# A hybrid encoder layer in fp32: the attention mask moves to one engine, and the order of copies, splits and tiles changes

## What is computed

```python
h = rmsnorm(x, mix_norm_g)
q, k, v, gb, gc, u = split(h @ w_in)                 # six parts of 512 columns
attn = dilated_attention(heads(q), heads(k), heads(v), slopes)   # 8 heads of 64
conv = gb * dwconv3(gc * u)                          # 512 channels, width 3
merged = concat([rmsnorm(attn), rmsnorm(conv)])
x = x + merged @ w_out
x = x + moe_ffn(rmsnorm(x), ...)                     # top 4 of 32 experts, clamped SwiGLU
return rmsnorm(x, final_norm_g)
```

## Time and profile before

| | us |
|---|---|
| median of 3 runs | 1372.1 |
| lowest and highest | 1367.39, 1372.46 |
| the profiled execution | 1373.16 |
| its span | 1371.3 |
| PE busy | 1317.0 (96%) |
| DVE busy | 504.3 (37%) |
| GpSimd busy | 267.0 (19%) |
| ACT busy | 205.0 (15%) |

### The profile page before, as it was taken

One profiled execution on the slowest core, in us unless ns is written; L12 is line 12 of the kernel. 1 busy time (PEld: TensorE's weight loads), 2 busy tenths in 40 slices (PEclk: granted clock), 3 DMA queues, 4 the chain that ended last, 5 costly groups with the idle time before them and its releaser, 6 DMA issues.

```text
span 1371.3 us, 33077 instructions
## 1 busy us (share of the span) xinstructions
PE 1317.0 (96%) x13998; PEld 647.4 (47%) x13998; DVE 504.3 (37%) x884; ACT 205.0 (15%) x313; POOL 267.0 (19%) x258
## 2 busy tenths in 40 slices
PE   6989999988999999999999999999999999999996
PEld 5766676882444444444444444444444434444443
DVE  7456653561233222222333333322222222333335
ACT  5134433230001000000010000100000000110002
POOL 1825427024011111111111111111111111111100
PEclk9999999979999999999999999999999999999998
DMA  9322113566999999999999999999999999999984
GB/s 245 82 62 62 62 62 105 223 236 226 348 398 406 403 408 400 402 410 407 402 403 407 398 402 407 412 407 406 404 406 406 407 408 404 409 408 402 406 354 143
DMA packets 94605, 450.79 MB, mean 329 GB/s; under 512 B 12105, under 2 KB 36953, under 8 KB 45424
## 3 DMA queue, kind: packets, MB, share of 16 engines
q1 hardware_dynamic: 83280, 426.27, 77.7%
q0 software_dynamic: 8656, 19.51, 5.9%
q10 hardware_dynamic: 2640, 4.59, 0.9%
HBM read 440.08 MB, written 18.67 MB: 335 GB/s over the span
## 4 chain that ended last, share of the span: by engine, by line
PE 76%; DMA 9%; DVE 5%; issue 4%; POOL 2%; SPq 2%; ACT 1%; DVEq 0%; POOLq 0%; ACTq 0%
PE gu_bank L1551 40%; PE bank L1565 21%; DMA raw<-in_w_gate_up_dram 9%; PE bank L1316 3%; PE bank L1318 3%; PE bank L1317 3%; PE bank L1539 2%; SPq L385 2%; PE bank L1393 1%; DVE probs_a L1030 1%; PE bank L1407 1%; PE bank L1518 1%; PE bank L1568 1%; DMA x_sb<-in_x_dram 1%; DVE lo L955 1%
## 5 line engine op out<-in xcount | busy, mean ns | idle before, releaser
L1551 PE MATMUL gu_bank<-raw,xT 128*32 128x512 f32 x3072 | 341.2, 593 | 6.0 <-DMA raw<-in_w_gate_up_dram 3.1
L1212 DVE TENSOR_TENSOR gate_in<-gu_bank,b_gu 128x768 f32<-128x768 f32 x32 | 30.6, 958 | 571.1 <-PE gu_bank L1551 538.9
L1551 PEld LDWEIGHTS gu_bank<-raw,xT 128*32 128x32 f32 x3072 | 101.2, 110 | 238.9 <-issue 220.2
L1565 PE MATMUL bank<-raw_a,aT 128*32 128x256 f32 x2232 | 166.8, 380 | 0.0
L1568 PE MATMUL bank<-raw_a,aT 128*32 128x256 f32 x744 | 166.4, 380 | 0.0
L1551 PE MATMUL gu_bank<-raw_c,xT 128*32 128x512 f32 x1488 | 165.5, 592 | 0.0
L586 POOL DMA_INDIRECT sum_rows<-y_out,scatter_list x31 | 45.2, 1457 | 429.7 <-ACT y_out L852 429.7
L1237 DVE STREAM_TRANSPOSE aT<-lin_in 128x192 f32<-128x192 f32 x128 | 67.8, 532 | 143.4 <-PE bank L1568 142.3
L1565 PEld LDWEIGHTS bank<-raw_a,aT 128*32 128x32 f32 x2232 | 88.8, 110 | 62.0
L838 ACT ACTIVATE xT<-bank 128x384 f32<-128x384 f32 x66 | 28.9, 488 | 554.8 <-PE bank L1539 539.6
L1551 PEld LDWEIGHTS gu_bank<-raw_c,xT 128*32 128x32 f32 x1488 | 49.4, 110 | 110.3 <-issue 105.3
(11 more groups left out here) (240 smaller groups left out, 1628.8 us busy)
## 6 DMA issues: line engine op xcount, KB each, us to landing
raw<-in_w_gate_up_dram SPq DMA_DIRECT2D x128, 1024.0 KB
raw_c<-in_w_gate_up_dram SPq DMA_DIRECT2D x62, 1024.0 KB
raw_a<-in_w_down_dram SPq DMA_DIRECT2D x62, 1024.0 KB
raw_b<-in_w_gate_up_dram SPq DMA_DIRECT2D x32, 1024.0 KB
raw_b<-in_w_down_dram SPq DMA_DIRECT2D x32, 1024.0 KB
raw_e<-in_w_gate_up_dram SPq DMA_DIRECT2D x31, 1024.0 KB
raw_d<-in_w_down_dram SPq DMA_DIRECT2D x31, 1024.0 KB
raw<-in_w_in_dram SPq DMA_DIRECT2D x24, 512.0 KB, 5.2
```

What stands on the lines that cost most here:

```text
L1212: dve.tensor_tensor(gate_in[:, :, :], gu_bank[:, :, 0:QUARTER], gate_b, ALU.add)
L1551: ins = pe.matmul(gu_bank[c * GROUP:(c + 1) * GROUP, r, :], xT[:, i, r * GROUP:(r + 1) * GROUP], w[:, c], start=first, stop=last)
L1565: pe.matmul(bank_[c * GROUP:(c + 1) * GROUP, cols], aT[:, k, c * GROUP:(c + 1) * GROUP], w[:, at:at + QUARTER], start=first and r % 2 == 0 ...
```

## The change

- `near_ready` is gone. DVE does the whole mask: `count_branches` and `log_of(2)`, `log_of(3)`, one of them behind each of the first three takes of v. GpSimd's queue keeps the parameter loads, the biases and the convolutions.
- At p = 0, PE makes tile (4, 0) ahead of the first turns, tile (4, 1) within the turns of head 0, and nothing within those of head 1; DVE's takes follow that order.
- In the loop over pairs, ACT and DVE copy turned blocks of the first head ahead of the split of chunk s + 2. DVE's take of tile (s + 1, 0) stays between the two heads' copies for p > 0.
- Channels 0 and 1 are scaled and split into two tiles of their own, at 72 K over the probabilities of the odd heads, as soon as all turns are done: on ACT ahead of `take_pair(3)`, on DVE behind the take of tile (10, 1).

```diff
+        first_hi_m, first_lo_m = overlay(72 * K, ("first_hi_m", [P, 2, SEQ], F32R), ("first_lo_m", [P, 2, SEQ], F32R))
...
+        def m_hi(k):
+            return first_hi_m[:, k, :] if k < 2 else mT_hi[:, k, :]
...
 @@ gpsimd
-            pool.wait_ge(bits_ready, 3)
-            made(pool.tensor_scalar(seen_b[:, :], step16[:, :], 0, None, ALU.is_equal))
-            pool.wait_ge(near_ready, 2)
-            made(pool.tensor_tensor(seen[:, :], seen[:, :], seen_b[:, :], ALU.add))
-            made(pool.tensor_tensor(seen[:, :], seen[:, :], seen_c[:, :], ALU.add))
-
-            inv = HEAD_DIM ** 0.5
-            made(pool.tensor_scalar(log_m[:, :], seen[:, :], 0.0, MASKED, ALU.is_equal, ALU.mult))
-            for m in range(2, len(BRANCHES) + 1):
-                made(pool.tensor_scalar(seen_b[:, :], seen[:, :], float(m), math.log(m) * inv,
-                                        ALU.is_equal, ALU.mult))
-                pool.tensor_tensor(log_m[:, :], log_m[:, :], seen_b[:, :], ALU.add).then_inc(log_m_made, 1)
-                pool.wait_ge(log_m_made, m - 1)
...
             pool.wait_ge(params_loaded, 16 * 9)
+            pool.wait_ge(bits_ready, 3)
+            pool.wait_ge(log_m_made, 1)
...
 @@ scalar, in the loop over p
                 take(s, 1)
+                take_turned(2 * p)
                 split_front(s + 2)
-                take_turned(2 * p)
                 take_turned(2 * p + 1)
                 if p >= 2:
                     square_conv(p - 2)
+            act.wait_ge(probs_turned, HEADS * TT)
+            act.wait_ge(params_loaded, 16 * 9)
+            split_merged(0)
+            split_merged(1)
             take_pair(NA - 1)
...
-            for k in range(NA):
+            for k in range(2, NA):
                 split_merged(k)
...
 @@ vector
+            def count_branches():
+
+                did(dve.scalar_tensor_tensor(seen[:, :], step16[:, :], 0.0, seen[:, :], ALU.is_equal, ALU.add))
+                did(dve.tensor_tensor(seen[:, :], seen[:, :], seen_c[:, :], ALU.add))
+
+            def log_of(m):
+
+                did(dve.tensor_scalar(seen_b[:, :], seen[:, :], float(m), math.log(m) * inv, ALU.is_equal, ALU.mult))
+                if m == 2:
+                    did(dve.tensor_scalar(log_m[:, :], seen[:, :], 0.0, MASKED, ALU.is_equal, ALU.mult))
+                ins = dve.tensor_tensor(log_m[:, :], log_m[:, :], seen_b[:, :], ALU.add)
...
                     if s == 0:
                         (distances, near)[n]()
+                    if s == 1 and n < len(masks):
+                        masks[n]()
...
                 normalise(2 * p)
+                if p == 0:
+                    take(s, 1)
                 normalise(2 * p + 1)
-                take(s, 1)
+                if p == 0:
+                    take(s + 1, 0)
+                else:
+                    take(s, 1)
+                    dve.wait_ge(pair_ready, p)
+                take_turned(2 * p)
                 split_front(s + 2)
                 if p:
-                    dve.wait_ge(pair_ready, p)
-                take_turned(2 * p)
-                take(s + 1, 0)
+                    take(s + 1, 0)
                 take_turned(2 * p + 1)
...
             take(N_IN - 2, 1)
+            dve.wait_ge(params_loaded, 16 * 9)
+            split_merged(0)
+            split_merged(1)
             take(N_IN - 1, 0)
...
 @@ tensor
                 project(s, 1)
-                turn_probs(2 * p, s + 1, 0)
-                turn_probs(2 * p + 1, s + 1, 1)
+                if p == 0:
+                    project(s + 1, 0)
+                    turn_probs(0, s + 1, 1)
+                    turn_probs(1)
+                else:
+                    turn_probs(2 * p, s + 1, 0)
+                    turn_probs(2 * p + 1, s + 1, 1)
```

More of the change, by code:

```diff
@@ L20 @@
 from contextlib import ExitStack
+from functools import partial
 import math
@@ L220, in build @@
         ident_cleared, ident_made = sem("ident_cleared"), sem("ident_made")
-        near_ready, log_m_made, first_bias_ready = sem("near_ready"), sem("log_m_made"), sem("first_bias_ready")
+        log_m_made, first_bias_ready = sem("log_m_made"), sem("first_bias_ready")
         pool_step, dve_step, act_step = sem("pool_step"), sem("dve_step"), sem("act_step")
@@ L329, in conv_tile, with m_lo @@
             return [t for i in range(N_IN) if chunks[i][0] == "conv" for t in range(first_tile[i], first_tile[i + 1])][c]
+        def m_hi(k):
+            return first_hi_m[:, k, :] if k < 2 else mT_hi[:, k, :]
+        def m_lo(k):
+            return first_lo_m[:, k, :] if k < 2 else mT_lo[:, k, :]
         def splits_to(i):
@@ L719, in square_conv, with split_merged @@
                 act.activation(sq_sb[:, 1, :], merged[:, NA + c, :], ACT.Square).then_inc(sq_conv_ready, 1)
+            def split_merged(k):
+                if k >= NA:
+                    act.wait_ge(conv_ready, k - NA + 1)
+                act.activation(m_hi(k), merged[:, k, :], ACT.Copy, scale=g_merge[:, k:k + 1]).then_inc(mT_hi_ready, 1)
             def exponents(h):
@@ L927, in near @@
                 dve.wait_ge(bits_ready, 3)
-                dve.tensor_scalar(seen[:, :], absd[:, :], float(half[0]), None, ALU.is_le).then_inc(near_ready, 1)
+                did(dve.tensor_scalar(seen[:, :], absd[:, :], float(half[0]), None, ALU.is_le))
                 did(dve.tensor_scalar(seen_c[:, :], absd[:, :], float(half[1]), None, ALU.is_le))
-                dve.scalar_tensor_tensor(seen_c[:, :], step4[:, :], 0.0, seen_c[:, :], ALU.is_equal, ALU.mult)\
-                   .then_inc(near_ready, 1)
+                did(dve.scalar_tensor_tensor(seen_c[:, :], step4[:, :], 0.0, seen_c[:, :], ALU.is_equal, ALU.mult))
+            assert BRANCHES[2][0] // 2 >= SEQ
+            inv = HEAD_DIM ** 0.5
+            def count_branches():
[6 more added lines that the diff above has]
+                ins = dve.tensor_tensor(log_m[:, :], log_m[:, :], seen_b[:, :], ALU.add)
+                if m == len(BRANCHES):
+                    ins.then_inc(log_m_made, 1)
+                else:
+                    did(ins)
+            masks = [count_branches] + [partial(log_of, m) for m in range(2, len(BRANCHES) + 1)]
             def first_bias(h):
-                dve.wait_ge(log_m_made, len(BRANCHES) - 1)
+                dve.wait_ge(log_m_made, 1)
                 dve.scalar_tensor_tensor(bias_h[:, h, :], absd[:, :], -2.0 ** (-8.0 * (h + 1) / HEADS) * HEAD_DIM ** 0.5,
@@ L1396, in score, with turn_probs @@
                             ins.then_inc(scores_ready, 1)
-            def turn_probs(h, s, n):
+            def turn_probs(h, s=None, n=0):
                 pe.wait_ge(probs_ready, (h + 1) * TT)
                 for c in range(TT):
-                    if c == 2:
+                    if c == 2 and s is not None:
                         project(s, n, 0, KD // 2)
@@ L1409, in turn_probs @@
                     ins.then_inc(probs_turned, 1)
-                project(s, n, KD // 2, KD)
+                if s is not None:
+                    project(s, n, KD // 2, KD)
             pe.wait_ge(ones_made, 1)
@@ L1478, in _ @@
                                     slice(i * D_MODEL + n * 512, i * D_MODEL + (n + 1) * 512)
-                                ins = product(bank[b][:, :], mT_hi[:, k, q], mT_lo[:, k, q], hi01[:, s % 2, cols],
+                                ins = product(bank[b][:, :], m_hi(k)[:, q], m_lo(k)[:, q], hi01[:, s % 2, cols],
                                               lo01[:, s % 2, cols], c == 0 and i == 0, c == 1 and i == 1)
```

5 lines of the change are left out of this document (4 added, 1 removed).

## The result

The changed kernel takes 1357.1 us, the median of 5 runs (1355.49 to 1360.79), against 1372.1 for the kernel before in the same measurement. The ratio, of the means of five executions each (1357.6 and 1371.0), is 0.9902, with a 95% interval of 0.9885 to 0.9918: 13.4 us less (11.3 to 15.8); the medians lie 15.0 apart. Measured again it was 0.9890 (0.9873 to 0.9907). Forecast were 1359 us and a gain of 13.3. The profiled execution took 1355.49 us, the fastest of its five, and that of before 1373.16, near its slowest.

What follows compares the result with a forecast made beforehand. TensorE bounds the kernel, busy 1317.0 of 1371.3 us, so only its waits and slow clock pay. 1.3 + 1.5 + 5.5 + 4.5 + 1.5 - 1.0 = 13.3 us gained, forecast 1359 us, range 1353 to 1366.

Steps and rivals of the forecast that it cites:

- Mask on DVE: Tiles of v up to first scores: first_bias 1.0 us earlier, v wait 0.5 shorter, 0.2 of new waits; gain 1.3 us.
- Tile ahead of the first turns: Pair 0: the 4.1 us probs_a wait and 2.8 of slow clock go, 1.4 of leftovers come; gain 5.5 us.
- Copies ahead of splits: Pairs 1 to 3: of 5.1 us of pT waits 0.6 stays; gain 4.5 us, plus 1.5 of clock at p = 2.
- Two channels early: Tail: the 1.5 us mT_lo wait goes into a 3.3 us wait for channel 3's squares; gain 0, clock charge 1.0 us.
- The clock terms: Work lost at low clock, counted as saved: 1.5 us at first scores, 2.8 behind probs_a, 1.5 at p = 2.
- the tail's charge: Tail: 1.0 us charged for the clock falling behind the 3.3 us wait for channel 3's squares, bounds 0 and 1.7.
- (a): Only waits go; the clock falls anyway at the shorter wait, in head 1's bare turns and tail: 1363 us, chance 0.14.
- (b): Front: early parameter loads delay the second weight chunk, up to 4.0 us on split, near and v tiles: 1363, chance 0.06.
- (c): The front is hidden: the stream of expert loads sets the end and nothing comes back: 1372 us, chance 0.08.
- (f): Takes of v wait behind mask steps; PE waits 1 to 2 us at three tiles: 1365 us, chance 0.03.
- (d): Better: no clock loss in the tail, shorter convolution (+2), expert entry falls favourably: 1354 us, chance 0.12.
- (e): Slower: the starved stretch at the expert entry grows, 9.5 us per 24 matmuls more: 1380 us, chance 0.02.

Runs made afterwards that it cites:

- The doubled mask: Changed kernel with two more two-input 128x896 DVE steps, writing a spare tile, behind each of the first three takes of v: 1363.58 us, ratio 0.9940 to before.
- the late loads: Changed kernel with GpSimd's nine parameter loads held back until the mask is made, about 41 us: 1358.08 us, ratio 0.9893 to before.
- the first chip: Chip of the first four experiments (mask, tile and copies alone; everything but the early splits); the kernel before took 1360.96 us there.
- the run with DVE's convolution: Changed kernel with the convolution of channel 3 made by DVE in five steps instead of GpSimd in seven: 1355.01 us, ratio 0.9872 to before.
- Idle products: Changed kernel with channel 3's convolution on DVE, plus unread TensorE products filling router waits: 1352.83 us, ratio 0.9855; with five more later, 1350.71 us, 0.9842.

## Why the prediction was right, step by step

**Mask on DVE: right.** Forecast 1.3 us for the stage. The second scores come 1.86 us earlier, 0.23 of it from before the first product: 1.6. PE's wait for the take of v is 0.5 us shorter, as forecast, since the second step of `near` fell from 1.35 to 0.63 us; the allowed 0.2 us of PE waits at the tiles of v did not come. The doubled mask shows that the steps were free because they fitted, as the prediction argued.

**Tile ahead of the first turns: right, also in its leftovers.** From the second scores to pair 1 the length went from 36.07 to 28.61 us: 7.5, against 5.5 plus the 1.5 of slow clock. Forecast were 1.2 us of waits in the bare turns and 0.2 behind; the trace has 0.25, 0.44 and 0.12. The 1.2 was too much: PE went from wait to wait with work between, and the walk charged the whole distance from 85.3 to 86.5. The lines of after, PE waiting once for ACT and once for DVE, whose split (79.86) stands ahead of its copy (82.06):

```profile
79.86 2.29 DVE L974 TENSOR_TENSOR lo<-raw,hi 128x2048 fp32r<-128x2048 f32 x1 [1.30 <-ACT hi L671]
...
81.71 0.66 PE L1435 MATMUL bank<-ident,probs_b 128*128 128x128 f32 x4 [0.25 <-ACT pT L737]
82.06 0.68 DVE L1058 COPY pT<-bank 128x512 f32<-128x512 f32 x1
...
82.80 0.66 PE L1435 MATMUL bank<-ident,probs_b 128*128 128x128 f32 x4 [0.44 <-DVE pT L1058]
```

**Copies ahead of splits: right.** 6.3 us over three pairs against 4.5 + 1.5. The 0.6 us that was to stay at p = 2 stayed (0.57).

**Two channels early: the cost did not come.** Forecast was a wait of 3.3 us and a net cost of 1.0; the two traces of after have 2.3 us and a gain of 0.5 and of 0.05, so the term is off by 1.0 to 1.5 us. What was mis-sized is GpSimd's convolution, which I held fixed: its add, now later against DVE's split, took 2.33 us where it took 3.05 before, and the convolution ended 0.9 us sooner, counted from the last `attend`. All five traces with early splits and GpSimd's convolution have 2.32 or 2.33, all five without them 3.04 or 3.05.

```profile
210.16 2.33 POOL L509 TENSOR_TENSOR merged<-merged,tap 128x512 f32<-128x512 f32 x1
...
217.58 1.10 PE L1407 MATMUL bank<-ones,sq_sb 128*128 128x1 f32 x8 [2.31 <-ACT sq_sb L716]
```

The clock did fall behind that wait, from 218.4 to 221.9 us, and the 0.9 us wait for the sums, which stood in the same place before, took up half of it. But the fall is not new, as I took it to be. Before it came in the same tail, ahead of the squares:

```profile
223.87:227.28 3.41, 3.41 (x8) 2.73 (x9) 3.38 (x3) 1.62 (x1) 3.23 (x3) 0.50 0.00 0
```

It cost nothing there: PE reached the squares just as they were ready, and would have waited for them instead. Nor does the fall hang on the wait of 2.3 us. In the runs without the tile and with the doubled mask, whose tail is that of after, it came with PE busy and was over by 216.1 and 219.4 us, ahead of the squares at 223.2 and 224.5, and the wait for them was then 0.8 us and none. The row of the run without the tile:

```profile
212.68:216.09 3.41, 3.41 (x9) 2.65 (x9) 2.85 (x2) 1.50 (x1) 3.23 (x3) 0.50 0.28 118
```

Of the 14 traces one has no fall in the tail. That the ratios cannot tell this part from zero is shown by the run without it.

**The clock terms were read from one execution, and that was the weak step.** I booked 1.5 us at the first scores, 2.8 behind `probs_a` and 1.5 at p = 2 as if they belonged to the kernel. They don't: behind the same waits the clock stayed at full in other runs, behind the first in one trace of three and behind the last in two of three. The wait of 2.5 us for the first scores in the run with the tile alone, and that of 2.8 us at p = 2 in the run with the mask alone:

```profile
56.09:60.07 3.98, 3.98 (x21) 2.53 (x22) 1.81 (x5) 0.00 (x0) 3.72 (x6) 1.00 0.50 88
```

```profile
151.61:155.00 3.39, 3.39 (x18) 2.84 (x19) 0.69 (x1) 0.00 (x0) 0.00 (x0) 1.00 0.87 305
```

The same stretches of before stand at 0.57 and, at p = 2, at

```profile
155.13:158.60 3.47, 3.47 (x11) 2.83 (x12) 0.69 (x1) 0.00 (x0) 0.00 (x0) 0.57 0.78 302
```

Behind the 4.1 us wait it fell in all four kernels that have it, for 6.8 us in two and 3.4 us in the other two. So part of the 17.7 us between the two profiled runs is the throw of the clock, in the front and in the router stage, and the mean gain of 13.4 to 15.1 us holds less of it. An estimate: the three terms weighed by these counts are 1.5 x 2/3 + 1.5 x 1/3 + 2.2 (the mean work lost behind the 4.1 us wait in the four traces) = 3.7 us rather than 5.8. The edited stages of the two traces gained 1.6 + 7.5 + 6.3 + 0.5 = 15.9 us, and 2.1 less is 13.8, within the measured 13.4 to 15.1. The sum of the prediction came so near, at 13.3, because the tail's charge and the overstated leftovers leaned the other way by about as much. That part of its accuracy is luck; the waits and their sizes are not.

**Rivals.** (a), less gain since the clock falls anyway, is partly true: it fell in the tail, as it had before, and did not at the 1.4 us wait or in the bare turns. (b), up to 4 us, is out, since the ratio with the late loads, 0.9893, lies between the two of after (0.9890 and 0.9902) and no split starts sooner with them; (c) is out since each part carried its gain to the end; (f) by the takes in the trace of after. (d), better than forecast, came in the profiled execution (1355.49) and not in the median; the shorter convolution was its one part that held. (e): PE's starved stretch in the entry of the experts, 26 matmuls in 13.5 us after where before had 24 in 11.5, is in ten traces and missing in the four of the first chip, whatever the edit. The entry was 2.0 us longer in after, about 1.7 of them from the lower clock, and never grew by the 20 us that (e) needed. Its cause was not tried and stays open.

## What to carry to other kernels

When an engine's wait is to be filled, compare the step's cost with the pace of the steps around it, not with its idle share: DVE took 6.2 us of mask for nothing because each portion, with its take, came to about one tile's time, and doubling it cost 5 to 7 us. A split that is moved early earns only when the chain that ends last in the same place is shortened too; here that was a convolution on GpSimd: each edit alone was worth nothing that could be measured, both together about 3 us in the total (0.9872 against 0.9896, intervals that just overlap) and in their stage (53.62 against 56.69). Read a fall of the granted clock in one trace as a chance, not as a cost of the kernel, until a second run shows it.

## What was not expected of the hardware

- The same wait does not always bring the clock down: after 2.5 and 2.8 us of idling it fell in the trace of before and not in the two above. It also fell with no wait at all, at 206.9 us in the run with DVE's convolution, with PE busy on sums of 128x1 and then on products. The Trainium skill ("TensorE: Matmul & The Clock Gate", What's actually happening) says that the slow stretch at a kernel's start varies from run to run of the same kernel; the two traces of after show the same in the middle of a kernel: in the router stage the slow stretch was 13.7 us in one and 17.1 in the other.
- In the router stage, which the change did not touch, the stretch at half speed was 13.7 and 17.1 us long after the change, 20.5 us before it (285.3 to 305.8), and 23.9 us with the late loads. Idle products took it to 3.4. The row of the late loads, clock 0.50 throughout:

```profile
267.50:291.40 23.90, 21.35 (x99) 20.53 (x98) 19.32 (x68) 6.26 (x7) 7.90 (x4) 0.50 0.58 234
```
- One stage that no edit touched differed by 11 us and more between measurements: some 190 matmuls at the entry of the experts took 20.74 us in all four traces of the first chip, whatever the edit, and 31.6 to 34.0 us in the others, where PE got through some 20 matmuls in 10 us and more with no wait for another engine to blame.
